# Index products of a sparse-attention stage in four groups of two heads and two tiles, and MLA score products with the unturned pairs ahead of the turned ones

## The reference, cut to what matters

```
# DSA: 8 index heads of 64, one shared index key, top 64 keys of each query are kept
dots = einsum('bqhd,bkd->bqhk', qi, ki) * 64 ** -0.5
idx_score = einsum('bqh,bqhk->bqk', wi, relu(dots))      # then causal mask and top-k

# MLA: 16 heads; a part of 64 per head, and a rotary part of 32 with one shared key
q = concatenate([q_nope, q_rope]);  k = concatenate([k_nope, broadcast(k_rope)])
s = einsum('bqhd,bkhd->bhqk', q, k) * 96 ** -0.5          # then causal softmax, times v
```

## Time and profile before

| | us |
|---|---|
| three runs | 2726.36, 2731.41, 2732.51 |
| their median | 2731.41 |
| span of the profiled execution | 2727.5 |
| PE busy in it | 2651.0 |
| POOL busy | 1972.7 |
| ACT busy | 1386.9 |
| DVE busy | 1017.6 |

### The profile page before, as it was taken

How to read it: one execution, slowest core, us unless ns; L and a number is a source line. 1 busy time by engine, 2 the same in 40 slices (tenths; PEclk the granted TensorE clock), 3 DMA queues, 4 the chain that set the end, 5 groups by cost and what they waited for, 6 DMA issues and landing times.

```text
span 2727.5 us, 35975 instructions
## 1 busy us (share of the span) xinstructions
PE 2651.0 (97%) x15016; PEld 2269.8 (83%) x15016; DVE 1017.6 (37%) x1695; ACT 1386.9 (51%) x1666; POOL 1972.7 (72%) x432
## 2 busy tenths in 40 slices
PE   6999989999999999999999999999999999999998
PEld 4889977899888778888888888888888888877887
DVE  6868867543212452121124311212441121244312
ACT  3754544555544555454454544544544454445543
POOL 3767764787887738878875688887658878774885
PEclk8999989999999999999999999999999999999999
DMA  8869843555554526546553455554425555443553
GB/s 331 309 230 353 311 157 108 191 213 182 200 193 175 181 88 223 188 170 216 186 197 137 160 186 194 192 192 177 155 111 199 192 193 192 179 179 115 194 192 108
DMA packets 80390, 521.78 MB, mean 191 GB/s; under 512 B 8908, under 2 KB 9292, under 8 KB 24420
## 3 DMA queue, kind: packets, MB, share of 16 engines
q1 hardware_dynamic: 72884, 492.72, 49.9%
q10 hardware_dynamic: 7344, 26.74, 2.5%
HBM read 518.38 MB, written 1.05 MB: 190 GB/s over the span
## 4 chain that ended last, share of the span: by engine, by line
PE 89%; DVE 6%; ACT 2%; DMA 1%; issue 0%; POOL 0%; SPq 0%; DVEq 0%; ACTq 0%
PE acc L555 17%; PE acc L594 17%; PE mb L532 11%; PE cb L532 11%; PE cb L507 10%; PE cb L534 6%; PE mb L534 6%; PE mb L647 2%; PE acc L872 1%; DVE hT L1875 1%; PE acc L507 1%; PE cb L833 1%; PE mb L857 1%; PE cb L647 1%; ACT whi L1184 1%; DMA raw<-in_w 1%
## 5 line engine op out<-in xcount | busy, mean ns | idle before, releaser
L2512 POOL TENSOR_TENSOR wlo<-raw,whi 128x2048 fp32r<-128x2048 f32 x428 | 1972.5, 4621 | 731.4 <-ACT whi L1184 667.3
L1184 ACT ACTIVATE whi<-raw 128x2048 fp32r<-128x2048 f32 x428 | 818.4, 1915 | 582.5 <-PE cb L532 251.3
L555 PE MATMUL acc<-whi,ARR 128*128 128x512 f32 x1312 | 366.5, 391 | 0.0
L532 PE MATMUL cb<-hT,whi 128*128 128x512 f32 x1280 | 335.4, 393 | 0.0
L532 PE MATMUL mb<-hT,whi 128*128 128x512 f32 x1280 | 334.1, 393 | 0.1
L555 PEld LDWEIGHTS acc<-whi,ARR 128*128 128x128 f32 x1312 | 245.6, 188 | 53.0 <-issue 2.9
L507 PE MATMUL cb<-hT,whi 128*128 128x256 f32 x1536 | 281.1, 285 | 0.0
L594 PE MATMUL acc<-whi,hT 128*128 128x512 f32 x960 | 270.8, 390 | 8.7 <-DVE hT L1875 7.4
L532 PEld LDWEIGHTS mb<-hT,whi 128*128 128x128 f32 x1280 | 230.2, 189 | 43.9 <-issue 3.1
L532 PEld LDWEIGHTS cb<-hT,whi 128*128 128x128 f32 x1280 | 229.6, 189 | 40.5
L1944 DVE TENSOR_TENSOR cb<-cb,AR 128x512 f32<-128x512 f32 x80 | 56.0, 700 | 552.8 <-ACT AR L1192 552.7
(11 more groups left out here) (332 smaller groups left out, 3367.6 us busy)
## 6 DMA issues: line engine op xcount, KB each, us to landing
raw<-in_w SPq DMA_DIRECT2D x436, 1024.0 KB, 4.8
AR<-in_a ACTq DMA_DIRECT2D x35, 512.0 KB, 6.2
AR<-in_a SPq DMA_DIRECT2D x29, 512.0 KB, 5.7
z<-in_a ACTq DMA_DIRECT2D x16, 512.0 KB, 6.8
gb<-in_lng SPq DMA_DIRECT2D x12, 512.0 KB, 5.7
gb<-in_lnb SPq DMA_DIRECT2D x12, 512.0 KB, 6.5
gb<-in_normg SPq DMA_DIRECT2D x8, 512.0 KB, 7.6
x<-in_x SPq DMA_DIRECT2D x1, 1024.0 KB, 8.4
```

The source lines that it names most:

```text
L532: ins = pe.matmul(to[j], wh[:, w], hT[:, k, :], start=k == 0, stop=k == 7)
L555: ins = pe.matmul(acc[:, 2 * t + c, 0:c1 - c0], xs[y], a[:, kk * width + c0:kk * width + c1], start=first and kk == 0 and m == 0, stop=las ...
L1184: ac.activation(whi[i % NH][:, :], raw[u % NR][:, :], ACT.Copy).then_inc(*up(s_hi, ("hi", i)))
L2512: po.tensor_tensor(wlo[i % NH][:, :], raw[(i + NADA) % NR][:, :], whi[i % NH][:, :].bitcast(F32), ALU.subtract).then_inc(*up(s_lo, ("lo", i)))
```

## The change

In DSA the index products of two heads are issued as one group for both tiles. A group has four products: two heads of tile 0 with 128 keys into columns 0 to 127 of two banks, then the same heads of tile 1 with 256 keys into columns 128 to 383. A projection has four such groups beside it, one every twelve products, where it had eight, one every six. ACT applies one Relu of 384 columns per head. DVE still does one update per head and tile, now tile 0 and tile 1 of a head in turn, and a bank is free after the second. In MLA the four unturned products of a step come first and the four turned ones after them; the first product of a bank starts the accumulation and the last one ends it.

```diff
 # scores_of, MLA
-                                        start=True, stop=name.startswith("dsa"))
-                    if name == "mla":
-                        for i, o in zip(parts, to):
...
-                            ins = pe.matmul(o[:, j * 256:j * 256 + nk], m_qrT3[r:r + 32, g, t * 128:t * 128 + 128],
-                                            m_krT[r:r + 32, 0:nk], start=False, stop=True)
+                                        start=j == 0 or name != "mla", stop=name.startswith("dsa"))
...
+                if name == "mla":
+                    for j in range(2):
+                        for i, o in zip(parts, to):
...
+                            ins = pe.matmul(o[:, j * 256:j * 256 + nk], m_qrT3[r:r + 32, g, t * 128:t * 128 + 128],
+                                            m_krT[r:r + 32, 0:nk], start=False, stop=j == 1)
 # dsa on TensorE
-                    for i0 in range(0, 16, 2):
-                        kind = ("cb", "mb")[i0 // 2 % 2]
-                        to = [claim(bank(kind), (name, "i", i)) for i in (i0, i0 + 1)]
-                        for i in (i0, i0 + 1):
-                            hd, t = index_part(i)
...
+                    for g in range(4):
+                        kind = ("cb", "mb")[g % 2]
+                        to = [claim(bank(kind), (name, "i", 2 * g + o)) for o in range(2)]
+                        for t in range(2):
+                            q.wait_ge(*on(name, "qiT", t, 0))
+                            q.wait_ge(*on(name, "kiT", t, 0))
+                            for o in range(2):
+                                r = 64 * o
+                                ins = pe.matmul(to[o][:, 128 * t:128 + 256 * t], d_qiT3[r:r + 64, g, t * 128:t * 128 + 128],
+                                                d_kiT[r:r + 64, 0:128 + 128 * t], start=True, stop=True)
...
-                rows_units(hi2, *hk, ready, (name, "q"), last=True, beside=beside, every=6)
+                rows_units(hi2, *hk, ready, (name, "q"), last=True, beside=beside, after=0, every=12)
 # dsa on ScalarE
-                        to = view((name, "i", i))[:, 0:128 * (index_part(i)[1] + 1)]
+                        to = view((name, "i", hd))[:, 0:384]
...
-                index(range(8))
+                index(0, 1, 2, 3)
                 sum_out(d_q, "q", on(name, "qrope", 0), 0)
-                index(range(8, 12))
+                index(4, 5)
                 unit(h + 5)
-                index(range(12, 16))
+                index(6, 7)
 # dsa on VectorE
-                index(range(8))
+                index(0, 1, 2, 3)
                 rope_sum("q", 0, 16, (name, "qrope", 0))
-                index(range(8, 16))
+                index(4, 5, 6, 7)
...
-                    q.wait_ge(*on(name, "iadd", 15))
+                    q.wait_ge(*on(name, "iadd", 7, t))
```

More of the change, by code:

```diff
@@ L417, in steps @@
             return [((s, s + 1) if s % 2 == 0 and s < 16 else (), (s - 3, s - 2) if s % 2 and s > 2 else ()) for s in range(18)]
-        def index_part(i):
-            return i // 4 * 2 + i % 2, i // 2 % 2
         started = {"dsa0": 11, "dsa1": 11, "fox": 18, "mla": 9}
@@ L833, in scores_of @@
                         ins = pe.matmul(o[:, j * 256:j * 256 + nk], qs[name](hd)[:, t * 128:t * 128 + 128], ks[name](hd)[:, 0:nk],
-                                        start=True, stop=name.startswith("dsa"))
-                    if name == "mla":
-                        for i, o in zip(parts, to):
-                            t, h0 = order[name][i]
-                            hd, nk = h0 + 2 * j, 128 * (t + 1)
-                            g, r = turned_place(hd)
-                            ins = pe.matmul(o[:, j * 256:j * 256 + nk], m_qrT3[r:r + 32, g, t * 128:t * 128 + 128],
-                                            m_krT[r:r + 32, 0:nk], start=False, stop=True)
+                                        start=j == 0 or name != "mla", stop=name.startswith("dsa"))
                     if name == "fox":
@@ L848, in scores_of @@
                                             f_l[r:r + 64, 0:nk], start=False, stop=True)
+                if name == "mla":
+                    for j in range(2):
+                        for i, o in zip(parts, to):
+                            t, h0 = order[name][i]
+                            hd, nk = h0 + 2 * j, 128 * (t + 1)
+                            g, r = turned_place(hd)
+                            ins = pe.matmul(o[:, j * 256:j * 256 + nk], m_qrT3[r:r + 32, g, t * 128:t * 128 + 128],
+                                            m_krT[r:r + 32, 0:nk], start=False, stop=j == 1)
                 ins.then_inc(*up(s_mm, *[("full", (name, "s", i)) for i in parts]))
@@ L937, in index @@
                 def index():
-                    for i0 in range(0, 16, 2):
-                        kind = ("cb", "mb")[i0 // 2 % 2]
-                        to = [claim(bank(kind), (name, "i", i)) for i in (i0, i0 + 1)]
-                        for i in (i0, i0 + 1):
-                            hd, t = index_part(i)
-                            o, nk = 64 * (hd % 2), 128 * (t + 1)
-                            q.wait_ge(*on(name, "qiT", t, 0))
[L945 to L949, removed]
+                    for g in range(4):
+                        kind = ("cb", "mb")[g % 2]
+                        to = [claim(bank(kind), (name, "i", 2 * g + o)) for o in range(2)]
+                        for t in range(2):
+                            q.wait_ge(*on(name, "qiT", t, 0))
+                            q.wait_ge(*on(name, "kiT", t, 0))
[3 more added lines that the diff above has]
+                                                d_kiT[r:r + 64, 0:128 + 128 * t], start=True, stop=True)
+                        ins.then_inc(*up(s_mm, ("full", (name, "i", 2 * g)), ("full", (name, "i", 2 * g + 1))))
                         yield
@@ L1550, in sum_out, with index @@
                     copy(c3(dst, 2)[:, t, :], acc_t(t), (name, part, t), ("free", ((name, part), t)))
-                def index(parts):
-                    for i in parts:
-                        q.wait_ge(*on("full", (name, "i", i)))
-                        to = view((name, "i", i))[:, 0:128 * (index_part(i)[1] + 1)]
-                        ac.activation(to, to, ACT.Relu, scale=0.125).then_inc(*up(s_ac, (name, "relu", i)))
+                def index(*heads):
+                    for hd in heads:
+                        q.wait_ge(*on("full", (name, "i", hd)))
+                        to = view((name, "i", hd))[:, 0:384]
+                        ac.activation(to, to, ACT.Relu, scale=0.125).then_inc(*up(s_ac, (name, "relu", hd)))
                 index_out(0)
@@ L2329, in dsa, with index @@
                 chain()
[L2331 to L2344, removed]
-                index(range(8))
+                def index(*heads):
+                    for hd in heads:
+                        q.wait_ge(*on(name, "relu", hd))
+                        for t in range(2):
+                            w, nk = wsc[:, 8 * t + hd:8 * t + hd + 1], 128 * (t + 1)
+                            if hd == 0:
+                                q.wait_ge(*on("cm"))
+                            else:
+                                q.wait_ge(*on(name, "iadd", hd - 1, t))
+                            dv.scalar_tensor_tensor(out=d_wk3[:, t, 0:nk], in0=view((name, "i", hd))[:, 128 * t:128 + 256 * t],
+                                                    scalar=w, in1=(d_wk3 if hd else c3(cst("cm"), 2))[:, t, 0:nk], op0=ALU.mult,
+                                                    op1=ALU.add).then_inc(
+                                *up(s_dv, (name, "iadd", hd, t), *([("free", (name, "i", hd))] if t else [])))
+                index(0, 1, 2, 3)
                 rope_sum("q", 0, 16, (name, "qrope", 0))
-                index(range(8, 16))
+                index(4, 5, 6, 7)
                 rope_sum("q", 1, 16, (name, "qrope", 1))
```

## The result

| kernel | runs | median us | range of the runs | ratio to before, 95% interval |
|---|---|---|---|---|
| before | 7 | 2731.41 | 2726.36 to 2734.29 | |
| changed | 7 | 2724.32 | 2721.84 to 2725.42 | 0.9975 (0.9966 to 0.9984) |

What follows compares the result with a forecast made beforehand. PE was taken to bound the kernel, busy 97% of the span. Savings of 3.3 us in DSA and 3.2 in MLA sum to 6.5 off the 2731.4 us median: 2724.9 us, range 2719 to 2730.

Steps and rivals of the forecast that it cites:

- PE bounds: Whole kernel: PE is busy 97% of the span, so a microsecond off its row is worth one, barring new waits.
- A block costs 0.20 us once: PE's score and index blocks: about 0.20 us once, plus 0.22 or 0.44 per pair; mixed DSA block 0.85 us.
- The edges of a group: DSA index groups: PE leaving and re-entering the 128-row form costs 0.22 us per group; a new group costs 1.07 us.
- 3.3 us for DSA, 3.2 for MLA: Savings of the two parts: index groups in two DSA stages 3.3 us, eight MLA score steps 3.2 us.
- Turned pairs pack like unturned ones: MLA scores: a second turned pair on 32 rows adds only 0.22 or 0.44 us, so the part saves 3.2 us.
- the rival: MLA scores: the second turned pair costs a full block, the part saves only 1.6 us; 2726.5 us, chance 0.12.
- Nothing is handed back: PE's waits stay as they are; the rival, PE arriving early and waiting, gives 2728.2 to 2731.4 us, chance 0.11.
- The slack at the query accumulators: DSA, keys of tile 1: the copy ends at 926.2, PE claims at 927.2; slack falls from 1.7 to 1.0 us.
- The slower rival: DSA: the copy freeing the query accumulators comes late and PE waits; release at 933 gives 2736.5 us, chance 0.04.
- The median: Whole kernel: the 6.5 us saving, carried from the span to the median of 2731.4, gives 2724.9 us.

Runs made afterwards that it cites:

- forms_same: Kernel before, same order and groups, but index products read 128 rows and turned MLA products 64; scores not the reference's. 2722.46 us, one run.
- mla_64_rows: Changed kernel with turned MLA products over 64 rows, the other head's 32 key rows zero, so scores stay right. 2721.83 us, ratio 0.9969 to before.
- two_groups_mid: Changed kernel with two index groups of four heads, at products 16 and 40, ScalarE's cast between them. 2722.11 us, ratio 0.9971 to before.
- Both parts alone: Kernel before with only the new DSA index groups: 2729.26 us; with only the new MLA scores: 2726.07 us, ratio 0.9984.
- dsa_only: Kernel before with only the new DSA index groups, MLA scores as before. 2729.26 us, ratio 0.9994 to before.

## Why the prediction was right, point by point

- **PE bounds, so a microsecond off PE is one off the end.** Right. The stages lose 6.42 us, and 6.1 us are missing at the end of the span when counted from the first landmark.
- **A block costs 0.20 us once, plus 0.22 or 0.44 per pair.** Right. The mixed block of 128 and 256 columns, which no row showed, takes 0.85 us as taken. Two experiments isolate the 0.20 in MLA: taking the change of form away without moving anything (`forms_same`, 1.69 to 1.09, three changes) and taking away the last one (`mla_64_rows`, 1.28 to 1.09).
- **The edges of a group cost 0.22 us.** Right: 1.08 us per group against 1.07. With two groups the saving was 0.88 us per stage against 0.80, so a group that is saved may be worth 0.02 to 0.04 us more than I put.
- **Two prices where the runs fit one.** The prediction pays for a block and for the edges of a group. But each change of form costs PE about 0.20 us, and a group among 128-row products has one on entry and one on exit (0.654 - 0.22 = 0.43 us for both). Counted so, the change takes 8 changes of form out of each DSA stage (1.60 and 1.62 us) and 16 out of MLA (3.20 us), `forms_same` 24 out of MLA (4.78 us), `mla_64_rows` 8 more than the change (1.56 us), and `two_groups_mid` 4 more per stage (0.88 us): 0.20 to 0.22 us each.
- **3.3 us for DSA, 3.2 for MLA.** 3.22 and 3.20. Both parts alone give the same to 0.02 us.
- **Turned pairs pack like unturned ones.** Right, and the rival falls: 0.64 us against 0.65. What spoke for packing, that a single turned pair costs what a single unturned one does, was a good guide. The Trainium skill, "TensorEngine Tiling (Array Packing)", Key Properties, says that a change of mode drains TensorE and a mere change of tile does not. The traces agree, in both directions: two 32-row pairs behind each other take 0.64 us where two apart took 0.84, and turned pairs on 64 rows pay nothing extra even when they alternate with the unturned ones (1.09 us a step). What the rows show is the price; that a drain is what takes the time is the page's word.
- **Nothing is handed back.** Right; the waits of the earlier trace rows are unchanged.
- **The slack at the query accumulators shrinks from 1.7 to 1.0 us.** It shrank to 1.3. The copy ended later than my 926.2, but the whole stage also lies 1.5 us later in this profile. Measured from the start of the last group it ended after 5.14 us, where I had 5.4, and PE's claim came after 6.4 us, as I had. The terms that were too large are the ones ahead of the rope: the Relus end 1.83 us after that start, where I had 1.9, and the rope starts 0.96 us after them (925.14 us), where I had 1.1 for the two updates. From rope to the end of the copy it is 2.35 us, as before.
- **The slower rival.** Its mechanism is real, but needs a group twice as large at the end. There PE starts 0.68 us late in the stage, and the stage is 0.83 us longer than without the wait.
- **The median.** I carried the saving over from the span to the median: 2724.9 against 2724.32. That this fits within 0.6 us is luck, since the part of the program ahead of the change moves the profiles by up to 4.7 us. The span itself, forecast at 2721.0, was 2722.9, and the stages say that the missing 1.9 us are mostly the 1.54 us lost before the first changed instruction.

## What to carry to other kernels

Where TensorE bounds, count how often its products change between full, half and quarter rows of the array, and compare the distance between starts across such a change with the distance within one form. Ordering or merging products by form, or filling rows with zeros to keep one form, saves 0.2 us per change here. Merge only as far as the engines behind can follow: find the accumulator that the last group's queue frees, and place the last group so that this release stays ahead of PE. For an edit of 0.1% compare stages between landmarks of the chain, since the medians of whole runs could not tell it (`dsa_only`: 0.9984 to 1.0003).

## What was not expected

- A lone pair of 64-row products gains nothing over two full 128-row products in this kernel: 0.654 us against 0.45 at 128 columns, 0.828 against 0.88 at 256, edges included. The halves of the array pay from the second pair on, which adds only 0.22 or 0.44 us.
- Full float32 products on 128 rows pay next to no edge among the split ones: in `forms_same` six projection products between them take 1.37 or 1.38 us, where 6 x 0.2276 is 1.37. So the edge belongs to the form, not to the type.
- The two profiles furthest apart differ by 5.4 us, and it arises between 129 and 152 us, from later loads of one input and from the lower granted clock behind PE's longer wait. A stage of 20 to 60 us later on differs by 0.02 us.
